# Latent attention: the rotary partner rows copied by GpSimd's DMA queue instead of made by a TensorE product

## The reference, cut to what matters

```python
cq = _rms_norm(x @ w_dq, g_q)
q = (cq @ w_uq).reshape(bsz, seq, MLA_HEADS, QK_NOPE + QK_ROPE)
q_nope, q_pe = q[..., :QK_NOPE], _rope(q[..., QK_NOPE:], cos, sin)
ckv_full = x @ w_dkv
k_pe = _rope(ckv_full[..., None, KV_LORA:], cos, sin)[:, :, 0, :]
s = (einsum(q_nope, k_nope) + einsum(q_pe, k_pe)) * scale
def _rope(x, cos, sin):
    x1, x2 = jnp.split(x, 2, axis=-1)
    return jnp.concatenate([x1 * c - x2 * s, x1 * s + x2 * c], axis=-1)
```

## Time and profile before

| | |
|---|---|
| median of three runs | 1078.16 us |
| the three runs | 1077.88 to 1078.3 us |
| span of the profiled execution | 1076.8 us |
| PE busy | 1067.1 us, 99% of the span |
| DVE, ACT, GpSimd busy | 65%, 51%, 4% |
| this stage (rotary key copied to first probabilities used) | 299 to 333 us |

### The profile page before, as it was taken

How to read it: one execution, slowest core, us unless ns; L and a number is a source line. 1 busy time by engine, 2 the same in 40 slices (tenths; PEclk the granted TensorE clock), 3 DMA queues, 4 the chain that set the end, 5 groups by cost and what they waited for, 6 DMA issues and landing times.

```text
span 1076.8 us, 14947 instructions
## 1 busy us (share of the span) xinstructions
PE 1067.1 (99%) x5901; PEld 926.9 (86%) x5901; DVE 702.8 (65%) x788; ACT 550.3 (51%) x651; POOL 47.4 (4%) x87
## 2 busy tenths in 40 slices
PE   8999999999999999999999999999999999999998
PEld 7888888888998888888878888889998888888886
DVE  4778756566776765656586555555888767555563
ACT  5563644444468454444465444445756746444443
POOL 1001000000200100000010000001040100000000
PEclk9999999999999999999999999999999999999999
DMA  9864765554572486665557655654784357655521
GB/s 312 295 217 151 254 184 185 191 188 154 142 265 72 164 264 191 195 195 194 160 192 236 191 175 186 194 153 134 215 253 165 118 168 236 200 180 186 193 107 39
DMA packets 138975, 201.68 MB, mean 187 GB/s; under 512 B 9144, under 2 KB 112800, under 8 KB 138928
## 3 DMA queue, kind: packets, MB, share of 16 engines
q1 hardware_dynamic: 136000, 191.25, 55.5%
q0 software_dynamic: 2928, 9.79, 2.7%
HBM read 199.95 MB, written 1.06 MB: 187 GB/s over the span
## 4 chain that ended last, share of the span: by engine, by line
PE 96%; DVE 2%; ACT 1%; issue 0%; POOL 0%; ACTq 0%; DVEq 0%; POOLq 0%
PE up L1865 26%; PE up L1868 14%; PE acc L1876 12%; PE acc L1877 12%; PE acc L1879 12%; PE up L1816 2%; PE up L1817 2%; PE up L1818 2%; PE acc L2004 2%; PE acc L1996 2%; PE acc L1995 2%; PE up L1938 1%; PE acc L2346 1%; PE up L2186 1%; PE up L1842 1%; PE up L1852 1%
## 5 line engine op out<-in xcount | busy, mean ns | idle before, releaser
L1205 DVE TENSOR_TENSOR weight_lo<-raw,weight_hi 128x2048 fp32r<-128x2048 f32 (+4 forms) x184 | 411.3, 2239 | 110.0 <-ACT weight_hi L642 109.8
L642 ACT ACTIVATE weight_hi<-raw 128x2048 fp32r<-128x2048 f32 (+4 forms) x184 | 343.4, 1869 | 154.3 <-PE acc L1879 146.2
L1865 PE MATMUL up<-x_parts,weight_hi 128*128 128x512 f32 x1232 | 307.5, 391 | 0.0
L1865 PEld LDWEIGHTS up<-x_parts,weight_hi 128*128 128x128 f32 x1232 | 224.5, 188 | 42.2
L1868 PEld LDWEIGHTS up<-x_parts,weight_lo 128*128 128x128 f32 x1232 | 168.1, 190 | 12.0
L1876 PE MATMUL acc<-weight_hi,hh 128*128 128x512 f32 x448 | 175.3, 391 | 0.0
L1877 PE MATMUL acc<-weight_lo,hh 128*128 128x512 f32 x448 | 175.0, 391 | 0.0
L1868 PE MATMUL up<-x_parts,weight_lo 128*128 128x256 f32 x1232 | 171.8, 282 | 0.0
L1879 PE MATMUL acc<-weight_hi,hl 128*128 128x512 f32 x448 | 138.5, 390 | 0.0
L642 ACT ACTIVATE tmp_a<-up 128x512 f32<-128x512 f32 x52 | 31.0, 597 | 148.0 <-PE up L1868 148.0
L1879 PEld LDWEIGHTS acc<-weight_hi,hl 128*128 128x128 f32 x448 | 84.1, 188 | 17.9
(11 more groups left out here) (278 smaller groups left out, 1094.4 us busy)
## 6 DMA issues: line engine op xcount, KB each, us to landing
raw<-in_ff_w SPq DMA_DIRECT2D x64, 1024.0 KB, 5.5
raw<-in_ffn_w_down SPq DMA_DIRECT2D x22, 1024.0 KB, 4.9
raw<-in_ffn_w_gate SPq DMA_DIRECT2D x20, 1024.0 KB, 5.4
raw<-in_ffn_w_up SPq DMA_DIRECT2D x20, 1024.0 KB, 5.3
raw<-in_w_in SPq DMA_DIRECT2D x14, 1024.0 KB, 5.6
raw<-in_sc_w_in SPq DMA_DIRECT2D x11, 1024.0 KB, 8.6
raw<-in_w_out SPq DMA_DIRECT2D x6, 1024.0 KB, 5.9
raw<-in_sc_w_out SPq DMA_DIRECT2D x4, 1024.0 KB, 6.2
```

The source lines that it names most:

```text
L642: return nc.scalar.activation(dst, src, ACT.Copy, **kw)
L1205: return vec.tensor_tensor(dst, whole, high.bitcast(F32), ALU.subtract)
L1865: mm(bank.rearrange("p (a n) -> p a n", a=2), w_h[k], x_parts[:, k, :, :], start=k == 0, stop=k == KD - 1, skip_group_check=True)
```

## The change

The exchange matrix goes out of the constants, and the sign goes into the sine table. For each rotation GpSimd starts four DMAs, each of which copies 32 partitions of `pe_raw` onto the partner's partitions of a new buffer `pe_partner` (two buffers, a semaphore for each). It waits for ACT's copy, and from the third rotation on also for the rotation that last read the buffer. PE makes the rotary block of each UQ slab first, and has a counter after it, so that ACT may copy that block before the slab's other two blocks are done. PE's first scores wait for the rotations of the keys and the first head pair alone, the scores of heads 2, 4 and 6 for the rotation of their pair.

```diff
@@ GpSimd, behind the roots of the latents
+            for r in range(5):
+                pool.wait_ge(mla["pe"], r + 1)
+                if r >= 2:
+                    pool.wait_ge(mla["rotated"], r)
+                for q in range(4):
+                    dst, src = 32 * q, 32 * (q ^ 1)
+                    pool.dma_start(pe_partner[dst:dst + 32, r % 2, :], pe_raw[src:src + 32, r % 2, :])\
+                        .then_inc(mla[f"swapped{r % 2}"], 16)
@@ ACT
             for j in range(4):
-                act.wait_ge(slab_used, UQ + j + 1)
+                act.wait_ge(mla["product_ps"], TILES + j + 1)
                 if j:
                     act.wait_ge(mla["rotated"], j + 1)
                 copy(pe_raw[:, (j + 1) % 2, :], up[2 + j % 2][:, 0:TOKENS], scale=-QK_SCALE).then_inc(mla["pe"], 1)
+                act.wait_ge(slab_used, UQ + j + 1)
@@ DVE, rotate(r)
-                dve.wait_ge(mla["swapped"], r + 1)
+                dve.wait_ge(mla[f"swapped{r % 2}"], 64 * (r // 2 + 1))
-                then(vec.tensor_tensor(tmp_d[:, 0:TOKENS], acc[:, 3, 0:TOKENS], sin, ALU.mult))
+                then(vec.tensor_tensor(tmp_d[:, 0:TOKENS], pe_partner[:, r % 2, :], sin, ALU.mult))
@@ PE
-            def partner(r):
-
-                pe.wait_ge(mla["pe"], r + 1)
-                if r:
-                    pe.wait_ge(mla["rotated"], r + 1)
-                mm(acc[:, 3, 0:TOKENS], swap, pe_raw[:, r % 2, :], start=True, stop=True).then_inc(mla["swapped"], 1)
-
             for j in range(4):
                 weights(UQ + j)
-                if j >= 2:
+                if j == 1:
+                    pe.wait_ge(mla["pe"], 1)
+                elif j >= 2:
                     pe.wait_ge(mla["q_out"], j - 1)
+                up_block(up[2 + j % 2][:, 0:TOKENS], UQ + j, 2 * NOPE, UQ_COLS, KQ, parts=(hh, hl)).then_inc(mla["product_ps"], 1)
                 for f in range(2):
-                    up_block(up[j % 2][:, f * TOKENS:(f + 1) * TOKENS], UQ + j, f * NOPE, UQ_COLS, KQ, parts=(hh, hl))
-                up_block(up[2 + j % 2][:, 0:TOKENS], UQ + j, 2 * NOPE, UQ_COLS, KQ, parts=(hh, hl)).then_inc(slab_used, 1)
+                    ins = up_block(up[j % 2][:, f * TOKENS:(f + 1) * TOKENS], UQ + j, f * NOPE, UQ_COLS, KQ, parts=(hh, hl))
+                ins.then_inc(slab_used, 1)
                 if j == 0:
                     turn_latent(2)
-                if j < 3:
-                    partner(j)
@@ PE, mla_score and before it
+                if h >= 2 and h % 2 == 0 and tile == 0:
+                    pe.wait_ge(mla["rotated"], 3 + h // 2)
-            pe.wait_ge(mla["rotated"], 6)
+            pe.wait_ge(mla["rotated"], 3)
```

More of the change, by code:

```diff
@@ L70 @@
 ROWS = ROW_XBC_B + XT
-C_ID, C_TRI, C_AFTER, C_SWAP, C_COS, C_SIN = 0, 128, 256, 384, 512, 768
-C_ALL = 1024
+C_ID, C_TRI, C_AFTER, C_COS, C_SIN = 0, 128, 256, 384, 640
+C_ALL = 896
 def shape_constants():
@@ L85, in shape_constants @@
     h = ROPE // 2
-    for d in range(P):
-        src, sign = (d + h, -1.0) if d % ROPE < h else (d - h, 1.0)
-        c[src, C_SWAP + d] = sign
     inv = np.float32(10000.0) ** (-np.arange(0, ROPE, 2, dtype=np.float32) / np.float32(ROPE))
@@ L91, in shape_constants @@
     c[:, C_COS:C_COS + TOKENS] = np.cos(ang)
-    c[:, C_SIN:C_SIN + TOKENS] = np.sin(ang)
+    c[:, C_SIN:C_SIN + TOKENS] = np.where(i[:, None] % ROPE < h, -1.0, 1.0) * np.sin(ang)
     return c
@@ L186, in two_blocks @@
         after = cst[:, C_AFTER:C_AFTER + P]
-        swap = cst[:, C_SWAP:C_SWAP + P]
         cos = cst[:, C_COS:C_COS + TOKENS]
@@ L205, in two_blocks @@
         pe_raw = take(2 * TOKENS, 2, TOKENS)
+        pe_partner = take(2 * TOKENS, 2, TOKENS)
         g_q = take(Q_LORA)
@@ L272, in two_blocks @@
         glu = Sems("glu", "small_out summed gate hidden hidden_hi chunk")
-        mla = Sems("mla", "rows latent_ps sumsq rstd latent turned t_hi t_lo pe q_out swapped rotated k_ps k_out values")
+        mla = Sems("mla", "rows product_ps sumsq rstd latent turned t_hi t_lo pe q_out swapped0 swapped1 rotated k_out values")
         att = [Sems(f"att{i}", "scores negmax probs normed turned t_out o_ps o_hi o_lo") for i in range(2)]
@@ L937, in _ @@
                     latent_hi(1, 2, 1)
-                act.wait_ge(mla["latent_ps"], 1 + tile)
+                act.wait_ge(mla["product_ps"], 1 + tile)
                 nc.scalar.activation((tmp_c, tmp_d)[tile][:, 0:KV_LORA], acc[:, 2 * tile + 1, 0:KV_LORA], ACT.Square,
@@ L961, in _ @@
                 if j < 3:
-                    act.wait_ge(mla["k_ps"], j + 1)
+                    act.wait_ge(mla["product_ps"], TILES + 4 + j + 1)
                 else:
@@ L2126, in _ @@
                     ins = key_latent(j, tile)
-                ins.then_inc(mla["latent_ps"], 1)
+                ins.then_inc(mla["product_ps"], 1)
             for j in range(2):
@@ L2157, in _ @@
                     ins = up_block(up[j][:, f * TOKENS:(f + 1) * TOKENS], UK, (2 * j + f) * NOPE, D, KKV, KQ)
-                ins.then_inc(mla["k_ps"] if j < 3 else slab_used, 1)
-                if j < 2:
-                    partner(3 + j)
+                ins.then_inc(mla["product_ps"] if j < 3 else slab_used, 1)
             def attention(i, score, scores_read, per_head_read, prob, v, s_bank, t_bank, o_dst, o_banks, own_banks=HEADS, masks=None):
```

## The result

The changed kernel takes 1083.12 us (median of five runs, 1082.49 to 1084.5), the kernel before takes 1078.3 beside it (median of five too); the ratio is 1.0047, with a 95% interval of 1.0036 to 1.0058. It is slower by 4.8 us. (One of the five runs of the kernel before took 1319.65 us, far from the other four, and is out of the ratio.) The profiled execution has a span of 1081.3 us and a time of its own of 1083.12.

The account below looks back on a forecast made before the run. DVE's line from rotation 3, not PE, was taken to bound the stage: +3.7 us, PE's 2.4 us saving hidden, takes the span from 1076.8 to 1080.5, plus 1.36 gives 1081.8 us; own range 1081.2 to 1082.5, over cases 1077.0 to 1083.3.

Parts of the forecast that it names:

- DVE's line: DVE's work without idle time from rotation 3 (315.66) to the first row maxima (322.33), 6.67 us, sets when L2178 starts.
- the load of WO+1 ... lands 7.1 us later: At rotation 1: the load, issued at 303.26 ahead of the four copies, lands at 310.36, the group at 310.5.
- E: End of rotation 1, forecast at 311.7 instead of 309.41; ACT's copy for rotation 3 waits for it.
- I take the load to be ahead: At rotation 3: WO+3's load precedes the fourth copy, the group lands with it at 319.3, rotation 3 starts 3.7 us later.
- rival 2: At rotation 3: the group gets ahead of WO+3's load and lands at 316.9, +1.3 us, time 1079.4; chance 0.2.
- Do the copies queue behind the loads?: GpSimd's copies stand behind loads that SP issued before them, landing some 0.18 us after the last load.
- Rival 1: Copies pass the loads: rotation 1's group lands at 308.5, rotation 3's 0.7 us earlier than before, time 1077.4; chance 0.17.
- PE's side: Five exchange products removed from PE save 2.4 us, the most the change can give, hidden under DVE's line.
- rival 3: PE's saving of 2.4 us comes whole, time 1075.8, if rotation 3 starts by 313.3; chance 0.04.
- The stall at UK: UK's second part waits for ACT's last query copies until 315.9, some 2 us, hidden under DVE's line.
- PE's clock is at full in all cases: PE is idle for a few us at most, so its clock stays at full in every case.
- Edits at no cost: Block order, sine product reading SBUF and relaxed score waits cost nothing on the way to the first row maxima.

## Why the prediction was right or wrong

**What bounds the kernel: right.** DVE's line sets the time. In the profiles of the change its lateness passes unchanged from rotation 1 to the row maxima, the transposes and the span (4.65, 4.60, 4.59, 4.5), held up at rotation 3 by the second group of copies, and the line and the median go together within 0.6 us in the change (+4.9 and +4.8) and in most experiments: -1.2 and -1.0 without copies, +1.4 and +2.0 with five buffers, -0.6 and -0.2 with all loads held. Two stand out: ACT's queue (+3.9 and +6.7), where rotation 0 too is late and PE waits for ACT, and the loads held in part (+2.1, and +4.5 in the median of runs).

**What failed first: "the load of WO+1 ... lands 7.1 us later".** The price of the copies was worked out from what loads do to a copy, and nothing was put down for what copies do to a load. The load takes 10.3 us, rotation 1 starts at 312.86 and not at 310.5, and E is 314.1 and not 311.7: 2.4 us too little, the largest error. (From the start of rotation 0, rotation 1 comes after 9.13 us, in the second trace and in that with the filled stall after 8.42 and 8.85; the forecast had 6.45.) The mechanism of this step held: group 1 and the load land within 0.4 us of each other, in these traces now the one and now the other first. The term that was mis-sized is the load's duration. That copies do this is shown by the run in which nobody reads them. That the group and WO+1's load are bound together is shown by holding the load (rotation 1 at 308.42).

**What failed second: "I take the load to be ahead".** The reason given held and the conclusion didn't: the load's issue did end first (316.68, against 316.80 for the fourth copy), and still that copy was there at 320.26, before the load near 322. Rotation 3's group went nearly as in rival 2, with 3.9 us for its last copy where that took 3.1. The forecast's own formula puts the landing 7.6 us behind E (319.3 - 311.7), rival 2's 5.2 us. Measured were 320.26 - 314.07 = 6.2. With the right E the forecast would thus have been 1.4 us too high, and the two errors partly cancel: 320.26 against the forecast's 319.3, hence a span of 1081.3 against 1080.5 and a time of 1083.12 against 1081.8 (the median stands 1.8 us above the span here, not 1.36). That the forecast is no further off is luck. The range over the cases (1077.0 to 1083.3) held the time by 0.2 us, and by a mixture of two cases; the forecast's own (1081.2 to 1082.5) didn't.

**Do the copies queue behind the loads?** Only partly. Group 1 beside WO+0's load alone lands in 3.0 us, with 54 packets moved from 303 to 306 us; with WO+1's load in flight too it moves none in that time (122 against 1 in the 3 us from the first issue). Rival 1 is false for groups 1 and 2. The rule of the Trainium skill (DMA: Bandwidth & Descriptors, section Queues, rings and completion order), that each DMA engine goes round between its queues, agrees with the first case (54 packets beside 252) and not with the second. What decides between them, no run here settles; where two held loads were released in the middle of a group (rotation 4's, 2.63 us of waiting), it was late again.

**PE's side: half right.** The saving of 2.4 us was taken to be hidden, and it was. But rival 3, that it comes whole, was not just unlikely: even with no copies at all the gain is about 1 us, since ACT's rounding of WO+0 is next. The stall at UK was put at 2 us at UK's second part; it is 3.08 us at the first, where PE waits for ACT's copy that waits for E. "PE's clock is at full in all cases" is wrong: the granted clock fell to half behind that stall. It cost nothing in the profiled execution, but it used up the cover: PE waited 4.2 us in all, not the 6 that the forecast gave.

**Edits at no cost: right.** Rotary block first and relaxed waits together, with the products kept: a ratio of 0.9999. Rotation 0's group hides.

## What to carry to other kernels

Before moving a small operation to DMA, price both directions: what the transfers under way do to it, and what it does to them. Here 4 copies of 32 KB took a 1 MB load from 7.1 to 10.3 us (8.9 to 10.3 in five traces). And ask of each result how long after its source it is due: copies hid where DVE came several us later (rotation 0), and cost 4.65 us where it came at once, and a buffer that is used in turn passed that lateness on to a group two rotations further. And take the operation out altogether as a first experiment, before building its replacement: it shows at once (about 1 us of 2.4) how much can be had at most.

## What the hardware showed that was not expected

- Copies of 32 KB within SBUF land 1.7 to 3.0 us after issue (medians of the groups in the run with all loads held), and 5.0 and 6.1 us in groups 2 and 1 of the changed kernel, with its loads ahead of them. ACT's hardware queue gave 5.3 us for group 1. In the prediction 3.1 us stood as the floor.
- Twenty such copies raise the median landing of the four 1 MB loads beside them from 5.0 to 8.7 us; five of 128 KB, the same bytes, raise it to 6.1 (one trace each).
- Behind a stall of 3.08 us PE was granted half clock from 314.5 to 321.3 us; in the same kernel again, behind 2.32 us, for some 3.4 us; with five buffers, behind 3.10 us, for some 3.3 us. Behind one of 3.04 us (loads held in part) and with a longest one of 1.6 us (filled stall) it kept full clock in this stage. So the length of the stall alone doesn't tell.
